# Decoder trunk on one core: the softmax probabilities are scaled on GpSimd in place of VectorE

## What is computed

```python
def block(i):                       # i = 0, 1: 128 queries each
    ...
    logits = jnp.einsum('bqhd,bqkhd->bhqk', qb, kg, preferred_element_type=f32) * (HEAD_DIM ** -0.5)
    logits = jnp.where(valid[:, None], logits, -jnp.inf)
    p = jax.nn.softmax(logits, axis=-1).astype(v.dtype)
    ob = jnp.einsum('bhqk,bqkhd->bqhd', p, vg)
    return ob.reshape(Bsz, Q_BLOCK, D)
```

## Time and profile before

| | us |
|---|---|
| median of three runs | 2449.76 |
| lowest and highest | 2448.98, 2450.52 |
| the profiled execution's own time | 2452.9 |
| its span in the trace | 2451.2 |
| TensorE busy | 2391.7 (98% of the span) |
| VectorE busy | 1857.8 (76%) |
| ScalarE busy | 1042.6 (43%) |
| GpSimd busy | 35.3 (1%) |

### The profile page before, as it was taken

How to read it: one execution, slowest core, us unless ns; L and a number is a source line. 1 busy time by engine, 2 the same in 40 slices (tenths; PEclk the granted TensorE clock), 3 DMA queues, 4 the chain that set the end, 5 groups by cost and what they waited for, 6 DMA issues and landing times.

```text
span 2451.2 us, 33454 instructions
## 1 busy us (share of the span) xinstructions
PE 2391.7 (98%) x12649; PEld 1923.6 (78%) x12649; DVE 1857.8 (76%) x2994; ACT 1042.6 (43%) x1245; POOL 35.3 (1%) x67
## 2 busy tenths in 40 slices
PE   7997899999999999999999999999999999999998
PEld 5584578878888888888878888778888888888886
DVE  8469969878878887898878987887777754455457
ACT  5353123464434444344454344555544334443442
POOL 0000000000000000000000000000000000000000
PEclk9998999999999999999999999999999999999999
DMA  9978748779989997898758877646788666666674
GB/s 376 398 253 314 285 166 310 248 230 344 311 284 310 341 306 264 292 331 299 254 167 291 290 250 228 203 138 191 254 293 288 220 196 189 189 189 191 195 218 144
DMA packets 311664, 627.39 MB, mean 256 GB/s; under 512 B 26608, under 2 KB 27024, under 8 KB 311504
## 3 DMA queue, kind: packets, MB, share of 16 engines
q1 hardware_dynamic: 306576, 611.27, 73.9%
q0 software_dynamic: 4288, 13.90, 2.0%
q10 hardware_dynamic: 640, 0.08, 0.0%
HBM read 623.05 MB, written 2.10 MB: 255 GB/s over the span
## 4 chain that ended last, share of the span: by engine, by line
PE 94%; DVE 2%; DMA 2%; ACT 1%; issue 1%; SPq 0%; DVEq 0%; ACTq 0%
PE psB L2217 42%; PE psA L2217 41%; DMA col_raw<-in_ada_w 2%; PE psT L1783 1%; PE psM L1815 1%; PE psA L2049 1%; PE psM L1826 1%; PE psT L2030 1%; PE psB L2030 0%; PE psT L1847 0%; PE psT L2019 0%; PE psA L2005 0%; PE psM L1796 0%; PE psM L1795 0%; DMA biasn<-in_ada_b 0%
## 5 line engine op out<-in xcount | busy, mean ns | idle before, releaser
L1155 DVE TENSOR_TENSOR w_lo<-w_raw,w_hi 128x1024 fp32r<-128x1024 f32 x732 | 893.1, 1223 | 465.5 <-ACT w_hi L807 461.0
L807 ACT ACTIVATE w_hi<-w_raw 128x1024 fp32r<-128x1024 f32 x732 | 774.8, 1060 | 1093.5 <-PE psB L2217 497.6
L2217 PE MATMUL psB<-w_hi,hT_hi 128*128 128x512 f32 x1040 | 407.3, 392 | 0.0
L2217 PE MATMUL psB<-w_hi,hT_lo 128*128 128x512 f32 x1040 | 404.9, 389 | 0.0
L2217 PE MATMUL psB<-w_lo,hT_hi 128*128 128x512 f32 x1040 | 404.7, 389 | 0.0
L2217 PE MATMUL psA<-w_hi,hT_hi 128*128 128x512 f32 x1008 | 397.6, 394 | 2.4 <-DVE w_lo L1155 2.1
L2217 PE MATMUL psA<-w_hi,hT_lo 128*128 128x512 f32 x1008 | 392.9, 390 | 0.0
L2217 PE MATMUL psA<-w_lo,hT_hi 128*128 128x512 f32 x1008 | 392.4, 389 | 0.0
L1172 DVE SCALAR_TENSOR_TENSOR ada_acc<-ada_raw,csil,ada_acc 128x512 f32<-128x512 f32 x465 | 347.5, 747 | 14.3 <-DVE ada_acc L1172 0.9
L2217 PEld LDWEIGHTS psB<-w_hi,hT_hi 128*128 128x128 f32 x1040 | 195.2, 188 | 45.9 <-issue 4.5
L2217 PEld LDWEIGHTS psA<-w_hi,hT_hi 128*128 128x128 f32 x1008 | 189.2, 188 | 49.1 <-issue 8.0
(11 more groups left out here) (376 smaller groups left out, 2316.8 us busy)
## 6 DMA issues: line engine op xcount, KB each, us to landing
w_raw<-in_ffn_w_in SPq DMA_DIRECT2D x352, 512.0 KB, 4.6
ada_raw<-in_ada_w SPq DMA_DIRECT2D x496, 256.0 KB, 5.5
w_raw<-in_ffn_w_out SPq DMA_DIRECT2D x176, 512.0 KB, 4.7
col_raw<-in_ada_w SPq DMA_DIRECT2D x128, 512.0 KB, 7.4
w_raw<-in_dsa_in_w SPq DMA_DIRECT2D x112, 512.0 KB, 4.6
w_raw<-in_s_glu_w SPq DMA_DIRECT2D x56, 512.0 KB, 5.7
w_raw<-in_s_in_w SPq DMA_DIRECT2D x32, 512.0 KB, 7.8
w_raw<-in_dsa_out_w SPq DMA_DIRECT2D x32, 512.0 KB, 5.0
```

The costliest lines, as they stand in the source:

```text
L807: nc.scalar.activation(high(u), w_raw[:, u % RING], ACT.Copy).then_inc(w_hi_ready, 1)
L1155: V.tensor_tensor(low(u), w_raw[:, u % RING], high(u).bitcast(F32), ALU.subtract).then_inc(w_lo_ready, 1)
L2217: ins = MM(PS[s][:, t, 0:r.width], a_[:, kt, tok], b_[:, kk, 0:r.width], start=kt == begin and m == 0, stop=kt == (end or r.units * UK) - ...
```

## The change

VectorE keeps the reciprocal, which now raises a new semaphore `inverse_ready`. The multiplication leaves VectorE's list. A loop over all 32 items is put into GpSimd's list where it comes to the run of the attention's output projection; each item waits for its reciprocal and multiplies in place, with the same operands, and raises `p_ready`, for which TensorE waits as before. A second new semaphore, `pT_other`, is declared and not used. The other engines' code is as it was.

```diff
+        lg_read, inverse_ready, pT_other = sem("lg_read"), sem("inverse_ready"), sem("pT_other")
...
                     pool.wait_ge(y_full, len(PIECES))
+                if r.before == "attention":
+                    for b in range(TOK * HEADS):
+                        N = (b // HEADS + 1) * P
+                        pool.wait_ge(inverse_ready, b + 1)
+                        nc.gpsimd.tensor_scalar(prob[b % 4][:, 0:N], prob[b % 4][:, 0:N], soft[:, b % 4, 3:4], None, ALU.mult
+                                                ).then_inc(p_ready, 1)
...
-                    if a >= 2:
+                    if 2 <= a < A + 2:
                         b = a - 2
                         vec.wait_ge(exp_done, b + 1)
-                        V.reciprocal(soft[:, b % 4, 3:4], soft[:, b % 4, 2:3]).then_inc(dve, 1)
-                        chain[0] += 1
-                        inverse = chain[0]
-                    if a >= 2:
-                        b = a - 2
-                        N = (b // HEADS + 1) * P
-                        vec.wait_ge(dve, inverse)
-                        V.tensor_scalar(prob[b % 4][:, 0:N], prob[b % 4][:, 0:N], soft[:, b % 4, 3:4], None, ALU.mult
-                                        ).then_inc(p_ready, 1)
+                        V.reciprocal(soft[:, b % 4, 3:4], soft[:, b % 4, 2:3]).then_inc(inverse_ready, 1)
```

## The result

The changed kernel takes 2457.5 us in the median of seven runs, the kernel before 2450.41 in runs beside it: a ratio of 1.0033, with a 95% interval of 1.0023 to 1.0042 (5.6 to 10.3 us), so **slower by about 7.1 us** by the medians. (The intervals of these ratios are some 2 us wide to either side; differences in us are those of the medians, and the stage's length in the traces is the finer measure.) That is outside the 0.2% that the prediction called no change, and inside its range of 2449.3 to 2458.5. The likeliest case, +2.4 us, did not come; the slower rival did, and by more than its +6.0.

What follows compares the result with a forecast made beforehand. The prediction took a ring of waits in the attention stage as the bound, not a full engine. Terms 3.5 + 0.3 - 0.6 - 0.8 = +2.4 us on 2449.76 gave 2452.2 us, range 2449.3 to 2458.5.

Steps and rivals of the forecast that it cites:

- The likeliest case: Whole kernel: the multiplication on GpSimd costs +2.4 us, giving 2452.2 us; between +0.2 and +4.9 us, chance 0.58.
- the slower rival: GpSimd's multiplication takes twice VectorE's time, 574 and 708 ns: +6.0 us, 2455.8; with the slow entry, chance 0.28.
- What bounds the stage: Attention stage, 34.66 us: no engine fills it, so waits between engines bound it, and its growth moves the end equally.
- The two paths: 128-key items: a path over ScalarE and one over TensorE's queue, both 1.60 us for two items, each holding one multiplication.
- the ring: Attention stage: waits among engines holding one multiplication per two items; turns of 1.60 us (128 keys) and 2.31 (256).
- Entry: Wait from VectorE's reciprocal to GpSimd's multiplication: +0.08 us a turn, between +0.03 and +0.25.
- Exit: Wait from the multiplication's end to TensorE's transpose: +0.03 us a turn, between 0 and +0.07.
- Body: GpSimd's multiplication itself: 343 ns for 128 keys and 508 for 256, +0.06 and +0.15 us a turn.
- the way out: Last item's transpose, copy, product and first weight product: carries one more growth, +0.3 us.
- What VectorE gets back: Maskings late behind low parts of four heads, 256 keys: 0.21 us back four times, -0.8 us; nothing with 128 keys.
- The slack: 256-key turns: the multiplication ends some 0.07 us before TensorE is free, absorbing 0.07 a turn, -0.6 us.
- The moved transfers: Four norm rows queued behind GpSimd's multiplications till about 1615: hidden by some 120 us before their first reader, no cost.

Runs made afterwards that it cites:

- The product of two tiles: The changed kernel with GpSimd's multiplication written as tensor_tensor with the reciprocal's column repeated; ratio 1.0011, +2.7 us against the kernel before.
- the reordered kernels: Reciprocal and multiplication moved ahead of masking, exponential ahead of copy: kernel before 0.9989; changed kernel 0.9994, with repeated-column product 0.9987; all ratios against the kernel before.

## Why the prediction was right or wrong

**What bounds the stage: right.** The two paths of the earlier trace rows and the one of the earlier trace rows are the ring. The product of two tiles shows the factor, one body a turn, and the reordered kernels show that an order without these paths frees time while the engines do the same work.

**Entry: right.** +0.08 was forecast; reciprocal to multiplication is 0.25 instead of 0.20, +0.05. The memset of the earlier trace rows was the right neighbour and the issue of a transfer the wrong one.

**Exit: right and small.** 0.06 where 0.09 was taken.

**Body: wrong, and it is the step that failed.** "GpSimd's nearest operation, which reads and writes a tile, is the mask", with 343 and 508 ns taken and 398 and 618 as the high ends. It measured 602 and 922, half as much again as the high ends. The mask's 0.86 ns a column are those of a copy (0.83), and a multiplication by a scalar takes three times that. The high end had been made by doubling the columns, a guess at a missing fetch and not at a missing rate, so it could not hold. The fetch for which it stood is 75 ns.

With the measured terms the prediction's own sum goes like this: a turn grows by 0.05 + 0.31 + 0 = 0.36 with 128 keys and by 0.05 + 0.57 + 0 = 0.62 with 256; 8 x 0.36 + 8 x 0.62 = 7.8, with 0.6 at the way out and -0.6 and -0.8 as forecast, is +7.0 us. The stages differ by 7.45, of which 0.64 is the slow clock: 6.8. So the ring was right and the term that was mis-sized most is the body, by 0.26 and 0.41 us. That the sum comes so close is luck in part, for two smaller misses cancel in it: with 128 keys 2.9 us was due and 15.96 - 0.64 - 13.47 = 1.85 came, with 256 keys 5.0 - 0.6 - 0.8 = 3.6 was due and 22.50 - 18.18 = 4.32 came. The distances from one reciprocal to the one two items on show where (the item is the one at the end of the distance; items count from 0):

| item | 9 | 11 | 13 | 15 | 17 | 19 | 21 | 23 | 25 | 27 | 29 | 31 |
|---|---|---|---|---|---|---|---|---|---|---|---|---|
| before | 1.59 | 1.91 | 1.59 | 2.29 | 1.90 | 2.32 | 2.31 | 2.50 | 2.31 | 2.51 | 2.31 | 2.02 |
| changed | 1.96 | 1.98 | 1.96 | 2.30 | 2.29 | 2.93 | 2.94 | 2.94 | 2.93 | 2.93 | 2.94 | 2.60 |

**What VectorE gets back: wrong in size at both places.** With 128 keys the forecast said that nothing comes back. But a turn with a low part in it, 1.91 or 2.29 us before, grows by 0.07 or 0.01 where the others grow by 0.37 (items 11 and 15 against 9 and 13): the low parts take up some 0.6 us of what the body costs. Another 0.23 comes at the start, where the second reciprocal follows the first after 0.38 us in place of 0.61, since no multiplication stands between them on VectorE any more. With 256 keys the forecast had four times 0.21. The masking is late no more, as it said, but the items run in two interleaved rows of turns, and only two of the turns in the row of the table were stretched (2.50, items 23 and 27): they grow by 0.43 where the others grow by 0.62, so 0.4 us comes back and not 0.8.

**The slack: there, but of no use.** A turn with 256 keys was to grow by 0.62 less 0.07. It grows by 0.63 (2.31 to 2.94). From the multiplication's start to the transpose the growth is 0.98 - 0.47 = 0.51, which is 0.06 less than the body's, so the slack was there. But from the transpose to the logits TensorE now takes 0.72 us (1604.17 to 1604.89) where it took 0.67, a distance that the prediction held fixed, and that uses it up. Why it is longer no run shows.

**The moved transfers: right**, shown with the norm rows issued first.

**The slower rival: right in kind.** It put the body at 574 and 708 ns and the total at +6.0. The first is close to the measured 602; the second is short of 922 by 0.21 us, since it multiplied VectorE's time by two and VectorE's slope is flat. The Trainium skill's stricter sentence (page GPSIMD Engine Reference, section Key points, about twice as fast on VectorE) fits these runs far better than its milder one (section Engine selection, operations with one input roughly line-rate). For the copy the trace agrees with the milder one as far as it can be seen: 292 and 398 ns, beside 287 and 354 of VectorE's multiplication, for the runs have no copy on VectorE. For the multiplication by a scalar it disagrees: at 2.5 ns a column that is slower than the product of two tiles at 1.66, and its ratios to VectorE are 602 / 287 = 2.1 and 922 / 354 = 2.6.

**The chances.** 0.28 stood on slower and 0.70 on no change. The weight lay wrong because both masks were taken as a measure of arithmetic; that a missing scalar might mean a missing rate was in no bound. That the time still lies in the range is owed to its upper end, which went past the doubled body and left room for a mean body of some 0.8 us; it was 0.76. Two of the signs of being wrong that the prediction named stood in the profile: a body beyond 0.6 us, and a granted clock under 1.00 in the stage (0.96).

## What to carry to other kernels

Ask of a short step what ring of waits it stands in before asking which engine has room: an engine at 1% is no cheaper place if the step lies once in every turn, and an engine at 80% is spared little if it waits in every turn. Price an operation on another engine by a row of the same form of instruction, or bound it by several times a copy: on GpSimd a copy, a product of two tiles and a multiplication by a scalar stood as 1 to 2 to 3 for each column. And when a ring is found, change the order first: two swaps of instructions in two queues brought 2.8 us with no engine changed, and with the shorter form of the instruction they made the engine of the multiplication indifferent.

## What the runs showed of the hardware

- GpSimd's multiplication of a tile by a scalar took 528 and 850 ns for 128 and 256 columns with a constant, 603 and 926 with a scalar from memory for each partition; a product of two tiles, the tile with itself or with a repeated column, 400 and 614; a copy 292 and 398. Of the multiplications the form with one tile to read is the slowest.
- The two waits across GpSimd were short: 0.09 us from the reciprocal's end to the multiplication, 0.06 from its end to the transpose.
- TensorE's granted clock fell to its lower level for some 3 us in the second of two pauses of 1.2 us, with four products between them and dense products ahead, in one of three profiles of one and the same kernel, and cost 0.64 us.
